# Convolution taps moved from the first two heads to later heads' maxima, and the sums across heads moved ahead of each head's filler

## The chip, the cores and the metric

The kernel runs on one core of one Trainium2 chip. The metric is device time in microseconds (us) of one execution; lower is better. The engines named below are TensorE (PE in the profile, with its weight loads as PEld), VectorE (DVE), ScalarE (ACT), GpSimd (POOL) and SyncE (SP), which issues the DMAs.

## The reference, cut to what matters

Two model blocks follow each other on 512 tokens of width 1024. The first has two layers, and each begins with a mixer that does two things to the same input and joins the results:

```python
def hybrid_mixer(x, ...):
    proj = x @ w_in + b_in
    c_q, c_kv, k_r, u = ...
    y_att = mla_group(c_q, c_kv, k_r, ...)          # 8 heads
    y_conv = conformer_conv_group(u, ...)           # 512 channels
    return concatenate([y_att, y_conv], -1) @ w_o

def mla_group(...):
    for start in range(0, S, 128):                  # causal by chunks of 64
        s = q_nope @ k_nope.T + q_rope @ k_rope.T
        p = softmax(where(mask, s * scale, -inf))
        outs.append(p @ v[:, :end])

def conformer_conv_group(u, ...):
    h = a * sigmoid(g)
    h = causal depthwise conv(h, 31 taps) + dw_b
    return silu(layer_norm(h))
```

After the mixer a layer has a cross attention over 256 memory tokens and a gated feed-forward part. The second block has a modulated mixer and a mixture of 16 experts. The change touches only the stretch of each of the two layers in which the 8 heads of `mla_group` are computed.

## The kernel before, in words

Every engine has its own instruction list, written out by hand in the order in which the engine runs it, and the lists meet through counting semaphores. An instruction that waits holds back all that stands behind it in its engine's list. Nothing reorders the work: what the code says first is done first.

In the attention stretch a head h has four query tiles t of 128 rows. Its work goes around the engines like this:

- PE, `scores(h)` (L1432): four products into four PSUM banks. From head 1 on, tile t waits until ScalarE has read the same tile of the head before.
- DVE, `maximum(n)` (L3421, L3423, L3425): a memset of the masked corner, the row maximum, and its scaled negative. After the second tile of head h, DVE does `reciprocal(h - 1)` (L3433): the reciprocals of the softmax sums of the head before.
- ACT, `exps(h)` (L2538): the exponentials with their row sums.
- PE, `turn_probs(h, tiles)` (L1443): transposes of the probabilities; ACT `turned_probs` (L2558) copies them out of PSUM.
- PE, `sums_across(pair)` (L1454): spreads the reciprocals of two heads (2 x pair and the next) over bank 4. It waits for DVE's reciprocals of both heads. ACT copies the bank to `mixT` (L2573).
- PE, `values(h)` (L1466, L1471): probabilities times values, into the same bank 4. For even h it waits for that copy.
- DVE, `pair_out(pair)` (L3438, L3441): multiplies a pair's outputs by the copied reciprocals, two heads later.

PE computes scores two heads ahead: in its loop over h the list is turn, `scores(h + 2)`, a filler, turn, turn, values. The filler is work of another part that needs a place: `modulation_rows(i)` (L1495) in heads 1 to 3 of the first layer and 1 to 4 of the second (`RING_MODS` is 4 and 5), and in head 6 `memory_product(0)` (L1197), the first of the cross attention's key and value products. The rest of them, `memory_product(1)` onward, follows the last head. `modulation_turn` (L1524) and DVE's `modulation_out` (L3447) finish a modulation chunk.

DVE has a second job, the depthwise convolution: 4 channel tiles x 31 taps = 124 instructions (L3352, and L3349 for each tile's first tap), handed out by `convolve(n)` in spare places. Before the heads 77 of them are done, the last 14 without anything between (one behind the last rotated query, then `convolve(13)`); in the heads there is one behind each maximum but the first (31), and 8 + 8 come after the last head, around the last `pair_out`. PE's `conv_sum` (L1411) needs all 124; it stands behind `memory_product(5)`.

Of the kernel before, what the change touches and what calls it, by code (L numbers as in the profile page):

```python
# [24 lines left out]
ACT = mybir.ActivationFunctionType  # L25
# [166 lines left out]
def build(nc, A, out, debug=None):  # L192
    with ExitStack() as ctx:
# [6 lines left out]
        def signal(name, per):  # L200
            return Signal(sem(name), per)
# [12 lines left out]
        ps = [banks[:, i, :] for i in range(8)]  # L214
# [27 lines left out]
        def view(lo, *shape, of=None):  # L242

            n = int(np.prod(shape))
            v = (arena if of is None else of)[:, lo:lo + n]
            if len(shape) == 2:
                return v.rearrange("p (a b) -> p a b", a=shape[0])
            if len(shape) == 3:
                return v.rearrange("p (a b c) -> p a b c", a=shape[0], b=shape[1])
            return v  # L250
# [6 lines left out]
        mixT = view(MIX, KT, S)  # L257
# [129 lines left out]
        rec_mm, rec_ev = signal("reciprocals_spread", HEADS // 2), signal("reciprocals_out", HEADS // 2)  # L387
# [361 lines left out]
        def score_tile(t):  # L749
            return ps[(0, 1, 6, 7)[t]][:, 0:(t + 1) * P]  # L750
# [116 lines left out]
        def ffn_chunk(n):  # L867

            half_no, i = (n - N_FFN) // (HALF + KT), (n - N_FFN) % (HALF + KT)
            return (half_no, half_no * HALF + i, True) if i < HALF else (half_no, i - HALF, False)  # L870
# [260 lines left out]
        def _(pe):  # L1131
# [46 lines left out]
            for l in range(DEPTH):  # L1178
# [244 lines left out]
                def scores(h):  # L1423
                    pe.wait_ge(qrot.sem, qrot.at(l, h + 1))
                    for t in range(ST):
                        n = h * ST + t
                        if n == 0:
                            pe.wait_ge(kv_ev.sem, kv_ev.at(l, 12))
                            pe.wait_ge(kcopy.sem, kcopy.at(l, 1))
                        if n >= 4:  # L1430
                            pe.wait_ge(sc_exp.sem, sc_exp.at(l, n - 3))
                        pe.matmul(score_tile(t), qh[:, h, t * P:(t + 1) * P], kh[:, h, 0:(t + 1) * P],  # L1432
                                  start=True, stop=True).then_inc(sc_mm.sem, 1)

                def turn_probs(h, tiles):
                    for kt in tiles:
                        n = h * ST + kt
                        if n >= 2:
                            pe.wait_ge(pt_ev.sem, pt_ev.at(l, n - 1))
                        if kt == 0:  # L1440
                            pe.wait_ge(sc_exp.sem, sc_exp.at(l, h * ST + ST))
                        for t in range(kt, ST):
                            mm = pe.transpose(ps[2 + n % 2][:, t * P:(t + 1) * P],  # L1443
                                              probs[:, h % 2, t, kt * P:(kt + 1) * P], ident)
                        mm.then_inc(pt_mm.sem, 1)

                def sums_across(pair):
                    pe.wait_ge(sc_rec.sem, sc_rec.at(l, 2 * pair + 2))
                    if pair:
                        pe.wait_ge(pv_ev.sem, pv_ev.at(l, pair))  # L1450
                    by_head = stat[:, 3, :].rearrange("p (h t) -> p h t", h=2)
                    for t in range(ST):
                        for i in range(2):
                            mm = pe.matmul(ps[4][i * VD:(i + 1) * VD, t * P:(t + 1) * P], by_head[:, i, t:t + 1].broadcast_to([P, VD]),  # L1454
                                           ident, start=True, stop=True)
                    mm.then_inc(rec_mm.sem, 1)
# [26 lines left out]
                def modulation_rows(i, wm=None):  # L1483
                    if wm is None:
                        arrived(C_MOD + i)
                        wm = w(C_MOD + i, 0, KT, 512)
                    if i == 0 and l == 0:
                        pe.wait_ge(cond_ok, 2)
                    if i >= 1:
                        pe.wait_ge(mod_in.sem, mod_in.at(l, i))  # L1490
                    elif l >= 1:
                        pe.wait_ge(mod_in.sem, mod_in.at(l, 0))
                    for k in range(KT):
                        for g in range(4):
                            mm = pe.matmul(mod_row(l, i)[g * MOD_COLS:(g + 1) * MOD_COLS, 0:P], cond[:, k, :],  # L1495
                                           wm[:, k, g * P:(g + 1) * P], start=(k == 0), stop=(k == KT - 1))
                        if k == 0:
                            say_spent(mm)
                    mm.then_inc(mod_rows.sem, 1)
                    if i < RING_MODS[l]:  # L1500
                        give_back(1 if i + 1 < RING_MODS[l] else 1 + MOD_CHUNKS - RING_MODS[l])
# [32 lines left out]
                for h in range(HEADS):  # L1534
                    turn_probs(h, (0, 1))
                    if h + 2 < HEADS:
                        scores(h + 2)
                    if 1 <= h < RING_MODS[l]:
                        modulation_rows(h)
                    if h == HEADS - 2:  # L1540
                        pe.wait_ge(sc_exp.sem, sc_exp.at(l, (HEADS - 1) * ST + 1))
                        memory_product(0)
                    turn_probs(h, (2,))
                    if h % 2 == 0:
                        sums_across(h // 2)
                    turn_probs(h, (3,))
                    values(h)
                    if h < RING_MODS[l]:
                        modulation_turn(h)
# [112 lines left out]
                for n in range(N_FFN, SPLIT_CHUNKS):  # L1662
                    half_no, t, hidden_tile = ffn_chunk(n)
# [706 lines left out]
        def _(act):  # L2370
            A1 = nc.scalar.activation
# [36 lines left out]
            for l in range(DEPTH):  # L2408
# [143 lines left out]
                def turned_probs(h, tiles):  # L2552
                    for kt in tiles:
                        n = h * ST + kt
                        act.wait_ge(pt_mm.sem, pt_mm.at(l, n + 1))
                        if h >= 1 and kt == 0:
                            act.wait_ge(pv_mm.sem, pv_mm.at(l, h))
                        nc.scalar.activation(probsT[:, kt, kt * P:S], ps[2 + n % 2][:, kt * P:S], ACT.Copy)\  # L2558
                            .then_inc(pt_ev.sem, 1)

                act.wait_ge(kcopy.sem, kcopy.at(l, 1))
                exps(0)
                for h in range(HEADS):
                    if h + 1 < HEADS:
                        exps(h + 1)
                    turned_probs(h, (0, 1))
                    if h < RING_MODS[l]:
                        act.wait_ge(mod_rows.sem, mod_rows.at(l, h + 1))
                        A1(gates[:, h % 2, 0:P], mod_row(l, h)[:, 0:P], ACT.Copy).then_inc(mod_row_ev.sem, 1)
                    turned_probs(h, (2,))  # L2570
                    if h % 2 == 0:
                        act.wait_ge(rec_mm.sem, rec_mm.at(l, h // 2 + 1))
                        A1(mixT[:, h // 2, :], ps[4][:, :], ACT.Copy).then_inc(rec_ev.sem, 1)  # L2573
                    turned_probs(h, (3,))
                    if h == HEADS - 2:
                        memory_copy(0)
# [145 lines left out]
                for n in range(N_FFN, SPLIT_CHUNKS):  # L2722
                    half_no, t, hidden_tile = ffn_chunk(n)
# [440 lines left out]
        def _(dve):  # L3164
# [31 lines left out]
            for l in range(DEPTH):  # L3196
# [163 lines left out]
                def convolve(n):  # L3360


                    for _ in range(n):
                        some = [t for t in range(open_tiles[0]) if taps_done[t] < TAPS]
                        others = [t for t in some if t != last_tile[0]] or some
                        t = max(others, key=lambda t: (TAPS - taps_done[t], -t))
                        tap(t)
                        last_tile[0] = t
# [37 lines left out]
                for h in range(HEADS):  # L3406
                    dve.wait_ge(up_mm.sem, up_mm.at(l, h + 1))
                    V.tensor_tensor(qh[turn, h, :], ps[h][turn, :], rope_cs[turn, :], ALU.mult).then_inc(qrot.sem, 1)
                    convolve(1)
                convolve(13)  # L3410
                def centred(t):
                    V.scalar_tensor_tensor(out=mixT[:, CT + t, :], in0=ps[5][:, :], scalar=-1.0 / CW,
                                           in1=mixT[:, CT + t, :], op0=ALU.mult, op1=ALU.add).then_inc(ccen.sem, 1)
# [36 lines left out]
                for h in range(HEADS):  # L3450
                    if h >= 4 and h % 2 == 0:
                        pair_out(h // 2 - 2)
                    for t in range(ST):
                        maximum(h * ST + t)
                        if t == 1 and h >= 1:
                            reciprocal(h - 1)
                        if h or t:
                            convolve(1)
                    if 2 <= h < RING_MODS[l] + 2:
                        modulation_out(h - 2)  # L3460
                pair_out(HEADS // 2 - 2)
# [103 lines left out]
                for n in range(N_FFN, SPLIT_CHUNKS):  # L3565
                    half_no, t, hidden_tile = ffn_chunk(n)
# [451 lines left out]
```

## Time and profile before

| what | us |
|---|---|
| median of 3 runs | 2466.85 |
| lowest, highest | 2466.54, 2467.28 |
| the profiled execution's own time | 2467.34 |
| span of the profile | 2465.5 |
| PE, DVE, ACT busy in the span | 2408.1, 1245.4, 792.9 |

The profile is one execution; its times count from the span's start. The heads of the first layer lie between about 111 and 183 us, those of the second between about 885 and 959 us. An engine's timeline shows each instruction's start and duration, its line and operation, and in brackets how long the engine had been idle before it and who ended that. The chain of waits goes back from the last instruction through whatever released each step. A busy PE is not PE at its peak, since matmuls overlap and their ends are modelled.

### The profile page before, as it was taken

The page shows a single profiled execution, that of the slowest core. Times are in us where ns is not written, and L with a number is a line of the kernel's source. Part 1 is how long each engine was busy: PE and PEld are TensorE (multiplying, and loading weights), DVE is VectorE, ACT ScalarE, POOL GpSimd, SP SyncE. Part 2 cuts the span into 40 slices and gives each one's busy share as a digit, 9 for nine tenths or more (in the row PEclk, how much of TensorE's full clock was granted, in tenths as well). Part 3 has the DMA queues.
Part 4 walks back from the last instruction along what each step waited for, and adds up shares of the span by engine and source line. Part 5 has one row for each costly group of instructions (what it writes and reads, how often), then busy time and mean ns, then how long its engine had stood idle before and what let it go on. Part 6 is the DMA issues. An engine that isn't in the chain of part 4 may idle for free.

```text
span 2465.5 us, 35670 instructions
## 1 busy us (share of the span) xinstructions
PE 2408.1 (98%) x15406; PEld 1717.3 (70%) x15406; DVE 1245.4 (51%) x1826; ACT 792.9 (32%) x1284; POOL 173.6 (7%) x117
## 2 busy tenths in 40 slices
PE   9999999999999999999999999999999999999998
PEld 6566877888887757687788888787899754444332
DVE  6983746433336896455633434687566431112222
ACT  4452434212224343353422322526332431111111
POOL 0000000000000000000000000190344010000000
PEclk9999999999999999999999999999999989999999
DMA  4342222323334233322332332311100279999998
GB/s 171 98 172 102 71 101 69 94 86 104 103 110 140 65 136 138 103 69 86 103 97 82 105 95 83 96 70 69 37 3 3 112 303 426 427 427 427 427 427 341
DMA packets 248820, 380.70 MB, mean 154 GB/s; under 512 B 21946, under 2 KB 187095, under 8 KB 224983
## 3 DMA queue, kind: packets, MB, share of 16 engines
q1 hardware_dynamic: 248316, 378.31, 41.8%
q8 instruction: 122, 2.00, 0.3%
q14 instruction: 36, 0.29, 0.0%
q10 hardware_dynamic: 346, 0.11, 0.0%
HBM read 376.28 MB, written 2.10 MB: 153 GB/s over the span
## 4 chain that ended last, share of the span: by engine, by line
PE 86%; DVE 7%; DMA 4%; ACT 2%; issue 1%; SPq 0%; DVEq 0%; ACTq 0%
PE banks L1263 40%; PE banks L2242 11%; PE banks L1197 4%; PE banks L1752 4%; PE banks L1896 4%; PE banks L1246 2%; DVE arena L3352 2%; DMA ring<-in_w_gate 2%; PE banks L2088 2%; PE banks L1617 1%; PE banks L1250 1%; PE banks L1591 1%; DMA arena<-in_w_gate 1%; PE banks L2226 1%; PE banks L2188 1%
## 5 line engine op out<-in xcount | busy, mean ns | idle before, releaser
L2612 ACT ACTIVATE w_hi<-ring 128x2048 fp32r<-128x2048 f32 (+1 forms) x100 | 174.6, 1746 | 423.9 <-PE banks L1263 423.9
L1263 PE MATMUL banks<-ffn_x_hi,w_hi 128*128 128x512 f32 x640 | 249.0, 389 | 0.0
L1263 PE MATMUL banks<-ffn_x_lo,w_hi 128*128 128x512 f32 x640 | 249.0, 389 | 0.0
L1263 PE MATMUL banks<-ffn_x_hi,w_lo 128*128 128x512 f32 x640 | 249.0, 389 | 0.0
L3211 DVE TENSOR_TENSOR w_lo<-ring,w_hi 128x2048 fp32r<-128x2048 f32 (+1 forms) x96 | 198.6, 2069 | 76.6 <-ACT w_hi L2612 75.4
L3352 DVE SCALAR_TENSOR_TENSOR arena<-arena,taps 128x512 f32<-128x512 f32 x240 | 175.0, 772 | 1.1
L3572 DVE TENSOR_TENSOR squares<-gates,banks 128x512 f32<-128x512 f32 x44 | 30.3, 688 | 275.5 <-PE banks L1263 262.3
L1263 PE MATMUL banks<-ffn_hidden_hi,w_hi 128*128 128x512 f32 x352 | 138.4, 393 | 0.0
L1263 PEld LDWEIGHTS banks<-ffn_x_lo,w_hi 128*128 128x128 f32 x640 | 120.1, 188 | 25.1
L1263 PEld LDWEIGHTS banks<-ffn_x_hi,w_lo 128*128 128x128 f32 x640 | 120.1, 188 | 24.9
L1263 PEld LDWEIGHTS banks<-ffn_x_hi,w_hi 128*128 128x128 f32 x640 | 120.1, 188 | 24.8
L1263 PE MATMUL banks<-ffn_hidden_hi,w_lo 128*128 128x512 f32 x352 | 137.1, 389 | 0.0
L1263 PE MATMUL banks<-ffn_hidden_lo,w_hi 128*128 128x512 f32 x352 | 137.0, 389 | 0.0
L3968 DVE SCALAR_TENSOR_TENSOR gates<-gates,tap_rows,banks 128x512 f32<-128x512 f32 x16 | 12.0, 747 | 231.3 <-PE banks L2242 200.0
L2242 PE MATMUL banks<-arena,zT 128*64 128x512 f32 x448 | 104.6, 604 | 2.1 <-DMA arena<-in_w_gate 1.0
L2242 PE MATMUL banks<-ring,zT 128*64 128x512 f32 x432 | 98.3, 596 | 2.0 <-DMA ring<-in_w_gate 1.6
L1197 PE MATMUL banks<-arena,ring 128*128 128x256 f32 (+1 forms) x352 | 98.0, 438 | 0.0
L1197 PEld LDWEIGHTS banks<-arena,ring 128*128 128x128 f32 x352 | 66.6, 190 | 30.6 <-issue 24.3
L1896 PE MATMUL banks<-arena 64*64 64x64 f32 x2688 | 85.8, 219 | 0.7 <-ACT arena L2883 0.7
L1896 PEld LDWEIGHTS banks<-arena 64*64 64x64 f32 x2688 | 81.9, 135 | 5.0 <-issue 1.5
L2242 PEld LDWEIGHTS banks<-arena,zT 128*64 128x64 f32 x448 | 31.0, 138 | 66.4 <-issue 59.9
L1263 PEld LDWEIGHTS banks<-ffn_hidden_lo,w_hi 128*128 128x128 f32 x352 | 66.1, 188 | 14.0 <-issue 0.5
(571 smaller groups left out, 4693.8 us busy)
## 6 DMA issues: line engine op xcount, KB each, us to landing
ring<-in_ffn_w_in SPq DMA_DIRECT2D x88, 512.0 KB, 4.7
arena<-in_w_gate SPq DMA_DIRECT2D x28, 1024.0 KB, 20.3
arena<-in_w_up SPq DMA_DIRECT2D x28, 1024.0 KB, 20.7
ring<-in_w_gate SPq DMA_DIRECT2D x27, 1024.0 KB, 21.5
ring<-in_w_up SPq DMA_DIRECT2D x27, 1024.0 KB, 20.8
ring<-in_w_down SPq DMA_DIRECT2D x24, 1024.0 KB, 16.8
arena<-in_w_down SPq DMA_DIRECT2D x24, 1024.0 KB, 19.6
ring<-in_w_mod SPq DMA_DIRECT2D x18, 1024.0 KB, 6.7
```

The costliest lines, as they stand in the source:

```text
L1197: mm = pe.matmul(bank[0:m, 0:width], weights(k), rhs(k), start=(k == 0), stop=(k == n - 1))
L1246: pe.matmul(ps[outs[o]][:, :], weights(o, wp, k), rhs[0][:, k, :], start=(k == 0 and wp == 0), stop=False)
L1250: mm = pe.matmul(ps[outs[o]][:, :], weights(o, 0, k), rhs[1][:, k, :], start=False, stop=(k == KT - 1))
L1263: mm = pe.matmul(bank[:, :], weights(wp, k), rhs(rp, k), start=(k == 0 and wp == rp), stop=(k == n - 1 and wp == 1))
L1752: mm = pe.matmul(out, wt[:, k, :], z[:, k, :], start=(k == 0 and i == 0), stop=(k == KT - 1 and i == 2))
L1896: mm = pe.matmul(units_of(bank)[rows, un, :], lhsT(un, rows), rhs(un, rows), start=True, stop=True)
L2088: mm = pe.matmul(bank, w_parts[wp], r_parts[rp], start=(k == DH and wp == rp), stop=(k == DH - 1 and wp == 1))
L2242: mm = pe.matmul(out, tokens, weights[:, n * 512:(n + 1) * 512], start=first, stop=last)
L2612: nc.scalar.activation(hi[:, 0:m], raw[n % 2][:, 0:m], ACT.Copy).then_inc(f_hi.sem, 1)
L3211: ins = V.tensor_tensor(lo[:, 0:m], raw[n % 2][:, 0:m], hi[:, 0:m].bitcast(F32), ALU.subtract)
L3352: ins = V.scalar_tensor_tensor(out=acc, in0=x, scalar=c, in1=acc, op0=ALU.mult, op1=ALU.add)
L3572: V.tensor_tensor(whole, gates[:, t % 2, :], ps[2 * (t % 4) + 1][:, :], ALU.mult)\
```

## The change

It does two things. First, taps: `convolve(13)` ahead of the heads becomes `convolve(10)`; head 0 (three taps) and head 1 (four) lose the taps between their maxima; every head from 1 on gets two taps behind its four maxima. What is left after the last head falls from 8 + 8 to 6 + 6. The number of taps, 124, stays. Second, for heads 2, 4 and 6 `sums_across` moves up in PE's list, from behind the third transposed tile to right behind `scores(h + 2)`, which is ahead of the filler; ACT's copy of it moves up ahead of the copy of the modulation row. Head 0 keeps the old order.

```diff
@@ PE, loop over the heads
                     turn_probs(h, (0, 1))
                     if h + 2 < HEADS:
                         scores(h + 2)
+                    if h % 2 == 0 and h:
+                        sums_across(h // 2)
                     if 1 <= h < RING_MODS[l]:
                         modulation_rows(h)
                     if h == HEADS - 2:
                         pe.wait_ge(sc_exp.sem, sc_exp.at(l, (HEADS - 1) * ST + 1))
                         memory_product(0)
                     turn_probs(h, (2,))
-                    if h % 2 == 0:
-                        sums_across(h // 2)
+                    if h == 0:
+                        sums_across(0)
                     turn_probs(h, (3,))
                     values(h)
@@ ACT, loop over the heads
+                def sums_copy(pair):
+                    act.wait_ge(rec_mm.sem, rec_mm.at(l, pair + 1))
+                    A1(mixT[:, pair, :], ps[4][:, :], ACT.Copy).then_inc(rec_ev.sem, 1)
...
                     turned_probs(h, (0, 1))
+                    if h % 2 == 0 and h:
+                        sums_copy(h // 2)
                     if h < RING_MODS[l]:
...
                     turned_probs(h, (2,))
-                    if h % 2 == 0:
-                        act.wait_ge(rec_mm.sem, rec_mm.at(l, h // 2 + 1))
-                        A1(mixT[:, h // 2, :], ps[4][:, :], ACT.Copy).then_inc(rec_ev.sem, 1)
+                    if h == 0:
+                        sums_copy(0)
                     turned_probs(h, (3,))
@@ DVE, ahead of the heads
                     convolve(1)
-                convolve(13)
+                convolve(10)
@@ DVE, loop over the heads
                         maximum(h * ST + t)
                         if t == 1 and h >= 1:
                             reciprocal(h - 1)
-                        if h or t:
+                        if h >= 2:
                             convolve(1)
+                    if h:
+                        convolve(2)
                     if 2 <= h < RING_MODS[l] + 2:
                         modulation_out(h - 2)
                 pair_out(HEADS // 2 - 2)
                 reciprocal(HEADS - 1)
```

On PE, at head 6 of both layers (L1443 are the transposes, L1454 the sums across heads, L1197 `memory_product(0)`, L1466 the values):

```order
 L1443 MATMUL banks<-consts,zT 128x128 [waits probsT_ev]
 L1443 MATMUL banks<-consts,zT 128x128 x2
+L1454 MATMUL banks<-consts,stat 64x128 [waits pv_ev,sums_reciprocal]
+L1454 MATMUL banks<-consts,stat 64x128 x7
 L1197 MATMUL banks<-arena,ring 128x256 [waits slot1_loaded,scores_exp]
 L1197 MATMUL banks<-arena,ring 128x256 x7
 L1443 MATMUL banks<-consts,zT 128x128 [waits probsT_ev]
 L1443 MATMUL banks<-consts,zT 128x128
-L1454 MATMUL banks<-consts,stat 64x128 [waits pv_ev,sums_reciprocal]
-L1454 MATMUL banks<-consts,stat 64x128 x7
 L1443 MATMUL banks<-consts,zT 128x128 [waits probsT_ev]
 L1466 MATMUL banks<-arena 64x128 [waits probsT_ev,reciprocals_out]
```

The wait for the reciprocals now stands ahead of the memory product instead of behind it. Head 2 of both layers and head 4 of the second have the same shift around `modulation_rows`.

On DVE, the end of head 7 before (L3421 to L3425 are a maximum, L3352 a tap, L3438 and L3441 `pair_out(2)`, L3433 the last reciprocal, on which the fourth sums across heads waits):

```order
L3421 MEMSET banks 64x64
L3423 TENSOR_REDUCE stat<-banks 128x1
L3425 TENSOR_SCALAR stat<-stat 128x1
L3352 SCALAR_TENSOR_TENSOR arena<-arena,taps 128x512
L3438 TENSOR_TENSOR arena<-arena,banks 128x384
L3441 TENSOR_TENSOR arena<-arena,banks 64x128 x2
L3433 RECIPROCAL stat<-stat 128x4
L3352 SCALAR_TENSOR_TENSOR arena<-arena,taps 128x512 x8
```

and now (all line numbers are 7 higher):

```order
L3428 MEMSET banks 64x64
L3430 TENSOR_REDUCE stat<-banks 128x1
L3432 TENSOR_SCALAR stat<-stat 128x1
L3359 SCALAR_TENSOR_TENSOR arena<-arena,taps 128x512 x3
L3445 TENSOR_TENSOR arena<-arena,banks 128x384
L3448 TENSOR_TENSOR arena<-arena,banks 64x128 x2
L3440 RECIPROCAL stat<-stat 128x4
L3359 SCALAR_TENSOR_TENSOR arena<-arena,taps 128x512 x6
```

Two more taps stand ahead of the last reciprocal in this head, as in every head from 2 on.

## Rows read from the trace of the kernel before

**Rows 1.** The page's chain that ended last, share of the span by engine.

```profile
PE 86%; DVE 7%; DMA 4%; ACT 2%; issue 1%; SPq 0%; DVEq 0%; ACTq 0%
```

**Rows 2.** Chain of waits, first layer, heads 0 to 2: start us, us, what.

```profile
111.23 9.37 DVE arena L3352 x14
...
134.10 1.12 PE banks L1454 x16
135.24 0.61 ACT arena L2573
...
149.83 1.05 PE banks L1454 x16
```

**Rows 3.** Chain of waits, first layer, head 6: start us, us, what.

```profile
172.87 3.46 PE banks L1197 x16
...
176.54 1.05 PE banks L1454 x16
...
178.26 0.32 PE banks L1466
```

**Rows 4.** Timeline of PE, first layer, heads 0 and 1: start us, us, what, idle before.

```profile
119.84 2.40 PE L1432 MATMUL banks<-arena 128*128 128x128 f32 x8 [0.73 <-issue]
...
124.05 1.57 PE L1432 MATMUL banks<-arena 128*128 128x128 f32 x6
```

**Rows 5.** Timeline of DVE, first layer, heads 2 to 7.

```profile
131.91 0.11 DVE L3421 MEMSET banks<- 64x64 f32 x1
...
138.73 0.11 DVE L3421 MEMSET banks<- 64x64 f32 x1 [0.74 <-PE banks L1432]
...
153.36 0.17 DVE L3447 TENSOR_TENSOR mod<-banks,par 128x8 f32<-128x8 f32 x1 [1.39 <-PE banks L1524]
154.39 0.11 DVE L3421 MEMSET banks<- 64x64 f32 x1 [0.86 <-PE banks L1432]
...
160.43 0.55 DVE L3438 TENSOR_TENSOR arena<-arena,banks 128x384 f32<-128x384 f32 x1
...
161.60 0.11 DVE L3421 MEMSET banks<- 64x64 f32 x1
...
168.33 0.11 DVE L3421 MEMSET banks<- 64x64 f32 x1 [0.70 <-PE banks L1432]
...
175.45 0.18 DVE L3433 RECIPROCAL stat<-stat 128x4 f32<-128x4 f32 x1
```

**Rows 6.** Timeline of DVE, second layer, heads 3 to 7.

```profile
912.85 0.11 DVE L3421 MEMSET banks<- 64x64 f32 x1 [0.73 <-PE banks L1432]
...
927.48 0.17 DVE L3447 TENSOR_TENSOR mod<-banks,par 128x8 f32<-128x8 f32 x1 [1.40 <-PE banks L1524]
928.51 0.11 DVE L3421 MEMSET banks<- 64x64 f32 x1 [0.86 <-PE banks L1432]
...
951.31 0.18 DVE L3433 RECIPROCAL stat<-stat 128x4 f32<-128x4 f32 x1
```

**Rows 7.** Chain of waits, second layer, heads 6 and 7: start us, us, what.

```profile
952.40 1.05 PE banks L1454 x16
...
954.12 0.32 PE banks L1466
```

**Rows 8.** Stretches: A:B us, length, busy (count) of PE, PEld, DVE, ACT, POOL; PEclk, DMA share, GB/s.

```profile
127.00:131.00 4.00, 2.59 (x14) 1.55 (x12) 3.82 (x12) 1.25 (x5) 0.00 (x0) 1.00 0.77 267
131.00:135.00 4.00, 2.47 (x21) 1.43 (x20) 3.79 (x14) 2.20 (x6) 0.00 (x0) 1.00 0.02 6
...
1984.00:1986.00 2.00, 0.82 (x5) 0.73 (x5) 1.93 (x5) 2.00 (x5) 1.62 (x2) 0.50 0.94 385
...
1988.00:1990.00 2.00, 2.00 (x12) 2.00 (x11) 1.93 (x3) 0.69 (x3) 1.80 (x1) 0.55 0.37 49
```

**Rows 9.** Timeline of PE in the second block, between 1980 and 1992 us.

```profile
1980.31 3.96 PE L2166 MATMUL banks<-consts,gates 2*128 2x2 f32 x16 [1.99 <-ACT gates L2974]
1985.45 6.02 PE L2172 MATMUL banks<-consts 128*128 128x128 f32 x34 [1.18 <-DVE stat L3911]
```

## Prediction, made before the changed kernel was run

> **What bounds the kernel now.** I read the chain of waits first: PE holds 86% of it and DVE 7% [rows 1]. Most of what PE holds is steady matmul work that the change leaves alone, so what counts is who holds the chain in the two attention stretches. In the first layer it runs over DVE's 14 taps from 111.23 to 120.60, over the maxima of heads 0 and 1 with a tap between each two, to PE's first sums across heads at 134.10 [rows 2]. So DVE paces PE until there. From then on PE mostly holds the chain, and DVE waits for it: the reader is to see the bracketed idle times in DVE's timeline, 0.74 + 1.39 + 0.86 + 0.70 = 3.69 us from head 3 to head 7 of the first layer [rows 5]. In the second layer the 0.73 comes once, the pair 1.40 and 0.86 twice: 5.25 us [rows 6]. These waits are all the room that DVE has in the later heads. At head 6 the reader is to see that PE does `memory_product(0)` at 172.87, for 3.46 us, and that the fourth sums start behind it at 176.54 [rows 3], 1.1 us after DVE began the last reciprocal at 175.45 [rows 5]. That product is what hides DVE's lateness there.
>
> **Prices.** A tap in a run costs 9.37 / 14 = 0.67 us [rows 2]. A head of DVE with four taps lasts from 161.60 to 168.33 less 0.70 of idle: 6.03 us. `pair_out` takes from 160.43 to 161.60: 1.17 us [rows 5]. The four maxima and a reciprocal without taps are then 6.03 - 4 x 0.67 = 3.35 us. With two more taps a head costs 7.37 us.
>
> **The early heads, a gain.** Three fewer taps in the run end it at 118.6 instead of 120.6, but PE starts the first scores only at 119.84 [rows 4], so head 0's maxima begin at about 120.2, 0.4 us earlier. Without taps they take 3.3 us, to 123.5. Head 1's scores stand behind the first modulation rows and start at 124.05 [rows 4], so DVE waits until about 124.35, is done at 127.7, adds two taps and begins head 2 at 129.05, where it began at 131.91 [rows 5]. That is 2.9 us earlier, and since head 1's reciprocal follows two maxima later, the first sums start at about 131.2, not at 134.10 [rows 2]. ACT follows each maximum at once and isn't in the way. The second layer has the same rows 774.12 us later (154.39 against 928.51 [rows 5, 6]), so I use the first layer's times for both.
>
> **The later heads, a loss on DVE.** Twelve more taps lie between 129.05 and the last reciprocal: 8.0 us. DVE walks from there in steps of 7.37, with 1.17 for each `pair_out`: head 3 at 136.4, head 4 at 144.95, end of it 152.3. Now the moved sums count. Those of head 2 need the reciprocal of head 3, which DVE gives two maxima into head 4 (two maxima, a tap and the reciprocal: 2.1 us), so at 147.05. Before, from these sums at 149.83 [rows 2] to head 5's first maximum at 154.39 [rows 5] it took 4.56 us; now the modulation rows (1.9 us) and two transposes (0.3) follow behind the sums and the wait for ACT's copy (about 0.45, from the copy at 135.24 of 0.61 us [rows 2] less one transpose) is gone: 6.3 us. Head 5 starts at 153.35 and DVE waits 1.0 us for it. Then 153.35 + 7.37 + 1.17 = 161.9 for head 6, 169.25 for head 7, and 169.25 + 7.37 + 1.17 = 177.8 for the last reciprocal, which was at 175.45. In the second layer head 4 still has a filler behind its sums, so head 7 gets its scores 6.3 us after the sums at 161.9 + 2.1 = 164.0, at 170.3: the last reciprocal is at 178.85, or 952.97 on the second layer's clock, where it was at 951.31 [rows 6].
>
> **Where the lateness lands.** The fourth sums stand ahead of `memory_product(0)` now. PE comes to them at about 173, as it came to the product at 172.87 [rows 3], and stands still until 177.9: a wait of nearly 5 us (about 4 in the second layer) with nothing to do behind it, for the product, the transposes and the values are all in the same list. After it come the sums 1.05, the product 3.46 and three transposes 0.33, and the values of head 6 start at 182.7, not at 178.26 [rows 3]: 4.4 us later. In the second layer 953.05 + 4.84 = 957.9 against 954.12 [rows 7]: 3.8 us later. So the gain of 2.9 at the start and three copy waits of 0.45 are there, and are more than paid back. What follows the heads has the same lists, and PE paces it, so the 8.2 us stay. The taps left over, 12 with one `pair_out`, take DVE 9.2 us, under the five products of 3.46 ahead of `conv_sum`: no cost there, and the copy moved on ACT costs nothing since ACT only waits in that place.
>
> **TensorE's clock.** The trace of before has no wait of PE this long. It shows one of 1.99 us at 1980.31, followed by tiny products and another of 1.18 [rows 9], and the granted clock at 0.50, the level of 1.2 GHz, when work resumed at 1985.45; it is 0.55 on the mean from 1988 to 1990 [rows 8], so it rose at about 1989.8. Some 4.35 us at half clock cost 2.2 us. On the other side, between 127 and 135 PE was busy for 5.06 of 8 us, in pieces, and the clock stayed at 1.00 [rows 8]. The new waits are longer than the first of these and lie in denser work. Bounds: 0, and 4.4 for a fall in both layers. I take one fall, 2.2, midway, since neither row is clearly nearer. The Trainium skill's page "TensorE: Matmul & The Clock Gate", in "Part 1: The HAM clock gate", has the clock drop to 1.2 GHz when the engine has been idle and come back with sustained work. By that rule both long waits would be followed by a fall; it is the third rival.
>
> **The sum.** 8.2 + 2.2 = 10.4 us on the profiled execution's 2467.34; the median of the runs is 0.49 lower, so 2466.85 + 10.4 gives 2477.2.
>
> **Rivals.** First, DVE keeps up and the change is **faster**. The place is the last reciprocal: if it came before PE reaches the fourth sums, at 172.87 less the 2.9 us gained, nothing would be paid back, and each layer would keep 2.9 + 3 x 0.45 = 4.25 us: 2458.4. It decides from a reciprocal at 170.0 on. Against it: 129.05 plus the same work as before (175.45 - 131.91 - 3.69 = 39.85) is 168.9 without one added tap, and the twelve cost 8.0. For it only that the early gain may be larger than I read. Chance 0.05.
>
> Second, about **no change**: DVE loses all its waits and more of the taps run under them. With no idle at all the last reciprocal of the first layer comes at 168.9 + 8.0 = 176.9, and head 6's values 4.94 us later, a shift of 3.6. In the second layer head 2 began at 131.91 + 774.12 = 906.03, and DVE's work up to the last reciprocal is 951.31 - 906.03 - 5.25 = 40.03 [rows 6]; so it comes at 906.03 - 2.86 + 40.03 + 8.0 = 951.2, and the shift is 2.0 [rows 7]. Without a fall of the clock 5.6 us in sum make 2472.4. With another microsecond gained in the early heads it would be within the 0.2% (4.9 us, about what a measurement of this kernel can tell from no change). Chance of ending within it 0.12.
>
> Third, **the clock falls after both long waits**, and perhaps after the 2.4 us that PE waits at the sums of head 2 as well: 8.2 + 4.4 = 12.6, to 14.8 with one more: 2479.5 to 2481.7. Their length against the 1.99 us of before speaks for it [rows 9], the dense work around them, as between 127 and 135, against [rows 8]. Chance 0.25.
>
> **Numbers.** The forecast, late reciprocals with at most one fall, has 0.58. The range runs from 2471, a little under the second rival's price, to 2482, the top of the third; outside lie the first rival and the better half of the second. Faster 0.05, same 0.12, slower 0.83.
>
> **What would show it.** In the changed profile the first sums of each layer should start 2.9 us earlier, DVE should have one wait of 1 us (two in the second layer) from head 2 to head 7 instead of four and five, the sums of heads 2, 4 and 6 should each be released by L3440, with PE idle about 2.4, 1.8 and 4 to 5 us before them, and the values of head 6 should start 4 us late. It is wrong if PE's wait at head 6 is under 2 us, or if the time after the heads doesn't keep the shift.

## The result and the profile after

| | us |
|---|---|
| before, median of 4 runs | 2466.69 (2465.77 to 2467.28) |
| after, median of 4 runs | 2482.12 (2480.98 to 2484.11) |
| ratio, 95% interval | 1.0064 (1.0046 to 1.0081) |
| profiled execution of after, its span | 2484.11, 2482.3 |

The change makes the kernel slower by 15.4 us. The direction is the one forecast. The time lies just above the range of 2471 to 2482, and the 2477.2 are 5 us short.

The busy times hardly move. PE is busy for 5.3 us more than before, and DVE's time stands where it stood:

```profile
PE 2413.4 (97%) x15406; PEld 1724.5 (69%) x15406; DVE 1245.5 (50%) x1826; ACT 792.0 (32%) x1284; POOL 173.7 (7%) x117
```

So PE does the same instructions, some of them slower, and waits longer. The view of PE's waits says on what (columns: engine, tile and line, releaser; us in total, times, longest). Of before:

```profile
PE banks L1454 <- DVE stat L3433: 1.6, 3, 0.6
```

Of after:

```profile
PE banks L1454 <- DVE stat L3440: 20.2, 8, 4.8
```

All eight sums across heads now wait for a reciprocal, for 20.2 us in all. The next view, PE's timeline of after, first layer, shows where. Its rows answer to [rows 2, 3, 4].

```profile
119.68 2.40 PE L1432 MATMUL banks<-arena 128*128 128x128 f32 x8 [0.73 <-issue]
...
131.38 1.09 PE L1454 MATMUL banks<-consts,stat 128*64 128x128 f32 x16 [1.30 <-DVE stat L3440]
...
147.33 1.80 PE L1454 MATMUL banks<-consts,stat 128*64 128x128 f32 x16 [2.47 <-DVE stat L3440]
...
165.88 1.09 PE L1454 MATMUL banks<-consts,stat 128*64 128x128 f32 x16 [1.86 <-DVE stat L3440]
...
179.72 1.97 PE L1454 MATMUL banks<-consts,stat 128*64 128x128 f32 x16 [4.77 <-DVE stat L3440]
...
191.44 0.43 PE L1466 MATMUL banks<-arena 128*64 128x128 f32 x2
```

The first sums start 11.70 us after the first scores, where it was 14.26. Then PE stands still for 2.47, 1.86 and 4.77 us ahead of the sums of heads 2, 4 and 6. Two of these four sums last nearly twice as long as the other two, 1.80 and 1.97 us against 1.09. The second layer has the same three waits (its rows answer to [rows 7]):

```profile
932.28 1.69 PE L1454 MATMUL banks<-consts,stat 128*64 128x128 f32 x16 [2.46 <-DVE stat L3440]
...
950.83 1.09 PE L1454 MATMUL banks<-consts,stat 128*64 128x128 f32 x16 [1.86 <-DVE stat L3440]
...
965.75 1.09 PE L1454 MATMUL banks<-consts,stat 128*64 128x128 f32 x16 [4.15 <-DVE stat L3440]
966.77 5.38 PE L1197 MATMUL banks<-arena,ring 128*128 128x256 f32 x16
```

Here `memory_product(0)` (L1197) takes 5.38 us. The windows of after, in the columns of [rows 8], tell why such rows are long: PEclk, the share of TensorE's full clock that was granted, is the first number behind POOL's.

```profile
145.00:147.00 2.00, 0.00 (x0) 0.00 (x0) 1.87 (x7) 0.00 (x0) 0.00 (x0) 1.00 0.00 0
147.00:149.00 2.00, 1.67 (x16) 1.40 (x16) 1.91 (x7) 0.00 (x0) 0.00 (x0) 0.64 0.00 0
149.00:151.00 2.00, 2.00 (x42) 1.80 (x44) 1.93 (x5) 0.60 (x1) 0.00 (x0) 0.51 0.03 8
151.00:153.00 2.00, 2.00 (x43) 1.56 (x36) 1.48 (x3) 0.95 (x4) 0.00 (x0) 1.00 0.00 0
...
179.00:181.00 2.00, 1.28 (x12) 1.28 (x14) 1.96 (x6) 0.00 (x0) 0.00 (x0) 0.50 0.03 8
181.00:183.00 2.00, 2.00 (x11) 1.47 (x8) 2.00 (x4) 0.60 (x1) 0.00 (x0) 0.50 0.00 0
183.00:185.00 2.00, 2.00 (x6) 1.58 (x5) 0.61 (x1) 0.00 (x0) 0.00 (x0) 0.50 0.00 0
185.00:187.00 2.00, 2.00 (x11) 1.70 (x11) 0.00 (x0) 0.00 (x0) 0.00 (x0) 0.97 0.00 0
```

Ahead of head 2's sums PE is idle and the clock still granted in full; as work resumes it falls to 0.50, which is the level of 1.2 GHz. At head 6 it is at 0.50 by the time work resumes. It is back some 4 us after the resumption at head 2 and somewhat over 5 us at head 6. I call this a fall of the clock. What it lengthens is read from the chain of waits of after:

```profile
147.33 1.80 PE banks L1454 x16
149.13 2.79 PE banks L1495 x64
...
179.72 1.97 PE banks L1454 x16
181.69 5.35 PE banks L1197 x16
...
932.28 1.69 PE banks L1454 x16
933.97 2.90 PE banks L1495 x64
...
965.75 1.09 PE banks L1454 x16
966.84 5.31 PE banks L1197 x16
```

The same pieces at full clock stand in the chain of waits of `e8_fill_head6`, an experiment below that has this order and these taps, and no fall in the heads:

```profile
147.27 1.09 PE banks L1454 x16
148.37 1.88 PE banks L1495 x64
...
178.06 1.09 PE banks L1454 x16
179.15 3.65 PE banks L1197 x16
```

Against these the four falls add 1.62, 2.58, 1.62 and 1.66 us: 7.5.

To compare kernels I use the **length of the heads**: from the start of the first scores, the first L1432 row of a layer, to the end of its last L1466 row, the values of head 7. It is 191.44 + 0.43 - 119.68 = 72.19 us in the first layer of after. Before, it ended with this row of PE's timeline, so 182.83 - 119.84 = 62.99:

```profile
182.40 0.43 PE L1466 MATMUL banks<-arena 128*64 128x128 f32 x2
```

| | first layer | second layer | both, against before |
|---|---|---|---|
| before | 63.0 | 64.7 | |
| after | 72.2 | 72.3 | +16.8 |

The spans of the two profiles differ by 2482.3 - 2465.5 = 16.8 us too, so all of it comes from the heads (the medians of the runs are 15.4 apart). In all the profiles shown here the rest of the program, whose code no kernel changes but for the taps behind the heads, was between 2333 and 2344 us long in sum (the clock falls there too, not in the same places each time: it is 0.50 from 1760 to 1762 us in after and 1.00 over the same work in before, at 1742 to 1746), so totals can differ by several us for reasons outside the heads. The lengths of the heads are free of that.

### The profile page after: what moved, and what is told of

Read it like the earlier page. It is cut to its first block, busy times and chain, and to the rows that moved or that the text cites. A ratio compares the mean times of both kernels' runs of the same rounds, so it can differ in the third digit from the quotient of the medians.

```text
span 2482.3 us, 35670 instructions
## 1 busy us (share of the span) xinstructions
PE 2413.4 (97%) x15406; PEld 1724.5 (69%) x15406; DVE 1245.5 (50%) x1826; ACT 792.0 (32%) x1284; POOL 173.7 (7%) x117
## 4 chain that ended last, share of the span: by engine, by line
PE 86%; DVE 6%; DMA 5%; ACT 2%; issue 1%; SPq 0%; DVEq 0%; ACTq 0%
PE banks L1263 40%; PE banks L2244 10%; PE banks L1197 7%; PE banks L1754 4%; PE banks L1898 4%; DMA ring<-in_w_gate 3%; PE banks L1246 2%; PE banks L2090 2%; DVE arena L3359 1%; PE banks L1619 1%; PE banks L1250 1%; PE banks L1593 1%; DMA arena<-in_w_gate 1%; DVE stat L3430 1%; PE banks L2190 1%
## 5 line engine op out<-in xcount | busy, mean ns | idle before, releaser
L2619 ACT ACTIVATE w_hi<-ring 128x2048 fp32r<-128x2048 f32 (+1 forms) x100 | 174.6, 1746 | 423.9 <-PE banks L1263 423.9
L1263 PE MATMUL banks<-ffn_hidden_hi,w_lo 128*128 128x512 f32 x352 | 137.1, 389 | 0.0
L1197 PE MATMUL banks<-arena,ring 128*128 128x256 f32 (+1 forms) x352 | 101.5, 450 | 0.0
L1197 PEld LDWEIGHTS banks<-arena,ring 128*128 128x128 f32 x352 | 69.0, 197 | 32.0 <-issue 24.8
L1263 PEld LDWEIGHTS banks<-ffn_hidden_hi,w_hi 128*128 128x128 f32 x352 | 66.1, 188 | 14.0 <-issue 0.5
```

Of the source, the lines that this page charges most:

```text
L1197: mm = pe.matmul(bank[0:m, 0:width], weights(k), rhs(k), start=(k == 0), stop=(k == n - 1))
L1263: mm = pe.matmul(bank[:, :], weights(wp, k), rhs(rp, k), start=(k == 0 and wp == rp), stop=(k == n - 1 and wp == 1))
L2619: nc.scalar.activation(hi[:, 0:m], raw[n % 2][:, 0:m], ACT.Copy).then_inc(f_hi.sem, 1)
```

## The experiments

Theory: PE's waits cost about what the forecast says, and the clock's falls behind them cost nearly as much again. Rivals: the added taps alone, or the moved sums alone, do it; or the falls only accompany the waits and cost nothing of their own. A kernel's difference is against the runs of before that shared its chip: medians of 2468.32 (22 runs) for the first four, 2467.53 (15 runs) for the next four, 2466.82 (7 runs) for the last two.

**One part alone.** First the moved sums and their copy with before's taps, `e1_order_only`, against after:

```diff
-                convolve(10)
+                convolve(13)
@@
-                        if h >= 2:
+                        if h or t:
                             convolve(1)
-                    if h:
-                        convolve(2)
```

> The sums across heads and their copies ahead of the filler in heads 2, 4 and 6, with the taps where they were before. Theory (the place of the sums in PE's list costs by itself, for at head 6 the memory product no longer covers DVE's last reciprocal): PE waits 2.8 us at head 6 in each layer and about 0.5 us at heads 2 and 4, the three copy waits of 0.45 us go, 1.8 us later per layer, 3.7 us in all without the clock; if the clock falls after the wait at head 6, another 1.9 to 2.8 us per layer, 2470 to 2476. Rival (the moved taps alone are to blame, the order saves the copy waits): 2.7 us faster than before, 2464.

Measured: 2475.15 us (5 runs), ratio 1.0035 (1.0022 to 1.0048): 6.8 us slower. PE's timeline at head 6:

```profile
176.47 1.97 PE L1454 MATMUL banks<-consts,stat 128*64 128x128 f32 x16 [2.82 <-DVE stat L3440]
178.37 4.32 PE L1197 MATMUL banks<-arena,ring 128*128 128x256 f32 x16
```

The order is enough to make a wait at head 6, 2.82 us in each layer, and a fall behind each. So the moved sums lose even with the taps where they were. How much is not settled by this run alone: the heads of its profile are 10.5 us longer than before's, but it has two more falls, among heads 0 to 2, where its lists are those of before (the last section shows one).

Then the taps alone with before's order, `e2_taps_only`, against before:

```diff
-                convolve(13)
+                convolve(10)
@@
-                        if h or t:
+                        if h >= 2:
                             convolve(1)
+                    if h:
+                        convolve(2)
```

> The changed kernel's taps with the order of the sums from before. Theory: the last reciprocal is 2 us later as in the changed kernel, but the memory product covers all but 1 us of it and the modulation rows cover the wait of head 2; the first sums still start 2.9 us earlier; no wait is over 2.2 us, so no fall of the clock: first layer 0.2 us later, second 1.8 us earlier, 2465. Rival (late taps are the cause wherever the sums stand): at least half of the 15 us stays, over 2474.

Measured: 2465.83 us (10 runs), ratio 0.9998 (0.9988 to 1.0007): no difference. PE's timeline shows the cover at work, the product ahead of the sums:

```profile
173.25 3.62 PE L1197 MATMUL banks<-arena,ring 128*128 128x256 f32 x16
...
178.19 1.09 PE L1454 MATMUL banks<-consts,stat 128*64 128x128 f32 x16 [1.10 <-DVE stat L3433]
```

The later taps make DVE late, but the product hides all but 1.10 us of it, and about that much the early heads give back: the heads of both layers are 1.0 us longer than before's. The expectation that no clock would fall did not hold. One fall is in this profile, among heads 0 to 2 of the first layer, where the longest idle time of PE ahead of it is 1.30 us:

```profile
133.00:135.00 2.00, 1.78 (x12) 1.44 (x13) 1.93 (x5) 2.00 (x9) 0.00 (x0) 0.56 0.30 28
```

Each part by itself costs 6.8 and about 0 us, and both together 15.4: the taps make DVE late, and the order turns its lateness into waits.

**The place at head 6.** `e3_head6_late` is after with the sums and their copy of head 6 in the old place:

```diff
-                    if h % 2 == 0 and h:
+                    if h in (2, 4):
                         sums_across(h // 2)
@@
-                    if h == 0:
-                        sums_across(0)
+                    if h in (0, 6):
+                        sums_across(h // 2)
```

(and the same for `sums_copy`).

> The changed kernel with the sums and the copy of head 6 alone in their old place; heads 2 and 4 keep the new order. Theory: the waits of 4.8 and 4.2 us at head 6 shrink to 1.2 and 0.4 us and the clock doesn't fall there, while the wait of 2.5 us at head 2 and its fall (1.7 us per layer) stay: 1.5 us from the waits and 3.3 us from the clock over before, 2471 to 2472. Rival (heads 2 and 4 carry the loss too, through DVE being late for everything behind): 2476 or more.

Measured: 2472.17 us (10 runs, 2467.86 to 2478.93), ratio 1.0021 (1.0009 to 1.0034). That is 3.9 us over before in place of 15.4, so some 11 us hang on the sums of head 6; the lengths of the heads agree (133.9 us in both layers of this profile, 144.5 in after's). The fall at head 2 is still there, in both layers, behind 2.46 us of idle.

**The clock by itself.** The next three kernels are after with PE kept at work through a wait: products of a constant with itself, into columns of bank 5 that nobody reads, just ahead of the sums. They are shorter than the waits, so no sum starts more than 0.1 us later for them. `e4_fill_waits` has 9 ahead of head 2's sums and 16 ahead of head 6's:

```diff
+                    if h in (2, 6):
+                        pe.wait_ge(mod_in.sem, mod_in.at(l, min(h, RING_MODS[l])))
+                    for _ in range({2: 9, 6: 16}.get(h, 0)):
+                        pe.matmul(ps[5][:, 2 * P:3 * P], ident, ident, start=True, stop=True)
                     if h % 2 == 0 and h:
                         sums_across(h // 2)
```

> The changed kernel with products of a constant by itself ahead of the moved sums, 9 at head 2 and 16 at head 6 of both layers, written to columns of bank 5 that nobody reads; they run while PE would wait for the reciprocal and end before it. Theory (half of the loss is the clock): the sums start when they did, but PE's clock stays at 1.00, the sums take 1.05 us and the memory product 3.46 us, and about 8 us of the 15 go: 2474 to 2476. Rival (the wait alone is the loss, the clock's fall lies beside it): the time stays within 1.5 us of the changed kernel's, 2481 to 2483.

Measured: 2474.43 us (6 runs, four between 2472.30 and 2474.46 and two at 2482.49 and 2482.99), ratio 1.0038 (1.0021 to 1.0054). Work that computes nothing makes the kernel 9 us faster than after: 6.1 over before in place of 15.4. The rival, by which falls cost nothing of their own, falls. The profiled execution is one of the two long ones. Its heads, 139.0 us in both layers, are still 5.5 shorter than after's. It has no fall at heads 2 and 6 but one at head 4 of the first layer and one among heads 0 to 2 of the second, and its program behind the second layer's heads took 5 us more than after's.

`e8_fill_head6` has the same with `{6: 16}`.

> The changed kernel with 16 products of a constant ahead of the sums of head 6 alone (columns of bank 5 that nobody reads). Theory: the falls at head 6 go, 2.8 and 1.9 us, those after the wait of 2.5 us at head 2 stay: 2477 to 2478. Rival (the falls have nothing to do with the wait ahead of them): 2481 to 2483.

Measured: 2473.28 us (10 runs), ratio 1.0024 (1.0015 to 1.0034): 4 us below what was expected. The expectation left head 2's falls in; this profile shows none, though PE waited there for 2.46 us in both layers. PE's timeline around head 6 (L1541 are the added products; lines from the sums on are shifted by 4):

```profile
173.11 3.74 PE L1541 MATMUL banks<-consts 128*128 128x128 f32 x32
...
178.06 1.09 PE L1454 MATMUL banks<-consts,stat 128*64 128x128 f32 x16 [1.21 <-DVE stat L3444]
```

and its windows:

```profile
174.00:178.00 4.00, 2.85 (x26) 2.66 (x24) 3.91 (x10) 1.65 (x4) 0.00 (x0) 1.00 0.44 164
178.00:182.00 4.00, 3.94 (x30) 3.44 (x31) 3.95 (x7) 0.60 (x1) 0.00 (x0) 1.00 0.00 0
```

No clock falls in these heads, so their lengths, 68.0 and 69.1 us, tell what the waits alone cost, less what the early heads gain: 137.1 - 127.7 = 9.4 us. After has 16.8; the other 7.4 are the falls, as the rows above added up to 7.5. The median of the runs is only 5.7 us over before's, and the rest of the program is 4.2 us shorter in this profile than in before's (2333.5 against 2337.8), with some 10 us at 0.50 there against 17; so the medians don't price the falls, and the lengths of the heads do.

`e9_fill_head2` has `{2: 9}` alone.

> The changed kernel with 9 products of a constant ahead of the sums of head 2 alone, none at head 6. Theory (a wait of over 4 us is always followed by a fall of the clock, one of 2.5 us only in some executions): both falls at head 6 stay, 2.8 and 1.9 us, the waits stay as they are, and the time is 1 to 4 us under the changed kernel's on the same chip, well above the kernel with head 6 filled: 2478 to 2481. Rival (head 2's falls cost as much as head 6's): it comes down by half of what filling both did, to 2477 or less.

Measured: 2479.38 us (4 runs), ratio 1.0046 (1.0029 to 1.0063), 12.6 us over before. Both falls behind head 6's waits are there, both of head 2's are gone, and 2.8 of the 15.4 us with them. (One fall among heads 0 to 2 of the second layer is in this profile too.)

**The same kernel once more.** `e10_after_again` is after, unchanged, on another occasion.

> The changed kernel as it is, on the chip of the run that fills head 2, for a comparison on one chip and for a second look at where the clock falls. Theory: 2480 to 2483, both waits of head 6 followed by a fall again, those of head 2 perhaps. Rival (the falls of the first profile were chance at head 6 too): a wait of 4 us or more with the clock at 1.00 behind it.

Measured: 2482.17 us (4 runs), ratio 1.0058 (1.0043 to 1.0073). PE's timeline at head 2:

```profile
147.28 1.09 PE L1454 MATMUL banks<-consts,stat 128*64 128x128 f32 x16 [2.46 <-DVE stat L3440]
```

and at head 6:

```profile
179.05 1.42 PE L1454 MATMUL banks<-consts,stat 128*64 128x128 f32 x16 [4.15 <-DVE stat L3440]
180.40 5.03 PE L1197 MATMUL banks<-arena,ring 128*128 128x256 f32 x16
```

Both falls behind head 6 come again. Behind head 2's 2.46 us there is one in the second layer and none in the first, where it was in the profile above; a fourth is at head 4 of the first layer.

**The lateness removed.** If DVE's taps are what makes PE wait, fewer of them in the heads must make both orders fast, since the rest fits behind the heads. `e5_fewer_taps` has `e3_head6_late`'s order, no tap in heads 0 and 1, three a head in heads 2 to 5 and two in the last two:

```diff
-                        if h >= 2:
+                        if h >= 2 and t >= (1 if h < 6 else 2):
                             convolve(1)
-                    if h:
-                        convolve(2)
```

> The changed kernel with fewer taps in the heads: none in heads 0 and 1, three per head in heads 2 to 5, two in heads 6 and 7, the rest (34) behind the last head; the sums of heads 2 and 4 in the new place, those of head 6 in the old. Theory (the early gain is real and is paid back only by the taps that stand ahead of the reciprocals): DVE is ahead of PE from head 3 on, every sum finds its reciprocal there, the 2.9 us of the early heads, 0.9 us of the first sums and the copy waits of heads 2 and 4 are kept: 5.8 to 6 us per layer, 2455 to 2456; no fall of the clock. Rival (taps pushed behind the last head hold up the convolution's sum or the split of the mixed halves): the gain is lost there, 2463 to 2468.

Measured: 2455.59 us (5 runs), ratio 0.9949 (0.9936 to 0.9961): 11.9 us faster than before. DVE's timeline has the last reciprocal at 168.69, where PE now waits for nothing, and the 34 taps behind it in two runs:

```profile
168.69 0.18 DVE L3440 RECIPROCAL stat<-stat 128x4 f32<-128x4 f32 x1
168.78 11.32 DVE L3359 SCALAR_TENSOR_TENSOR arena<-arena,taps 128x512 f32<-128x512 f32 x17
...
181.20 11.35 DVE L3359 SCALAR_TENSOR_TENSOR arena<-arena,taps 128x512 f32<-128x512 f32 x17
...
198.67 1.89 DVE L3419 SCALAR_TENSOR_TENSOR arena<-banks,arena 128x512 f32<-128x512 f32 x3 [2.37 <-PE banks L1411]
```

Even so, DVE is ahead of `conv_sum` and waits 2.37 us for PE there.

`e6_fewer_taps_old_order` has these taps in before's order.

> The kernel before with the same fewer taps (ten ahead, none in heads 0 and 1, three per head in 2 to 5, two in 6 and 7, the rest behind the last head) and all sums in the old place. Theory: the early gain alone, 4.3 us per layer, 2458, and PE waits 0.44 us for the copy in each pair as before; the difference to the same taps with the moved sums, 2.5 to 3 us, is what the new place is worth when DVE is early. Rival (the new place is a loss by itself): this one is the faster of the two.

Measured: 2457.62 us (5 runs), ratio 0.9960 (0.9946 to 0.9974). With DVE early, the lengths of the heads put the new order of heads 2 and 4 ahead by 2.2 us (117.3 against 119.4); the two kernels' times, 2.0 us apart, overlap.

`e7_no_late_taps` is after with every sum in its new place, head 6's too, and three taps a head in heads 2 to 5 alone (`if 2 <= h < 6 and t >= 1`).

> The changed kernel with all its moved sums (head 6 too), no taps in heads 0, 1, 6 and 7, three per head in heads 2 to 5, the rest behind the last head. Theory: without taps in heads 6 and 7 the last reciprocal comes within half a microsecond of PE's arrival even ahead of the memory product, so the place of the sums that cost 4 to 5 us in the changed kernel costs nothing, 6 us per layer, 2454 to 2456. Rival (at head 6 the place is bad whatever DVE does, since pair_out stands ahead of the reciprocal): PE still waits over 1.5 us there and it is 3 us or more slower than with the sums of head 6 in the old place.

Measured: 2455.74 us (4 runs), ratio 0.9950 (0.9936 to 0.9964). PE's timeline at head 6:

```profile
168.20 1.09 PE L1454 MATMUL banks<-consts,stat 128*64 128x128 f32 x16 [0.56 <-DVE stat L3440]
```

So the place that cost some 11 us in after costs nothing to be measured when the reciprocal is there in time. All three kernels with fewer taps beat both before and after.

## Why the prediction was wrong in its time and right in its direction

- **The early heads.** A gain of 2.9 us was forecast; the first sums come 2.56 earlier. Head 1's first score tile and the way to its maximum took a little longer than the 0.30 that was taken. The chain of waits of after, head 1:

```profile
123.97 0.43 PE banks L1432 x2
124.40 0.07 issue
124.47 0.12 DVE banks L3428
```

- **The later heads.** PE's waits came out as the last part of the forecast has them: about 2.4, 1.8 and 4 to 5 us, each released by L3440, and measured 2.47, 1.86 and 4.77 (second layer 2.46, 1.86, 4.15). DVE's timeline of after, first layer, answers to [rows 5]:

```profile
154.14 0.17 DVE L3454 TENSOR_TENSOR mod<-banks,par 128x8 f32<-128x8 f32 x1 [1.66 <-PE banks L1524]
...
155.17 0.11 DVE L3428 MEMSET banks<- 64x64 f32 x1 [0.87 <-PE banks L1432]
...
179.49 0.18 DVE L3440 RECIPROCAL stat<-stat 128x4 f32<-128x4 f32 x1
```

  Four waits have become one place with two, 1.66 + 0.87 = 2.53 us where 1.0 was forecast, and the last reciprocal is 1.7 later than the 177.8 worked out. The fall at head 2, which the walk left out, stretches PE's sums and modulation rows by 1.62 us, and what DVE waits for comes behind them. Where no clock fell, `e8_fill_head6`, the sums of head 6 start at 178.06, against 177.9 forecast.
- **Where the lateness lands.** Right: in the idle time ahead of head 6's sums, with nothing behind it to do. `e2_taps_only` shows the cover that was there and `e3_head6_late` what its loss costs. The waits' term was 8.2 us; `e8_fill_head6` gives 9.4. The sums came back to the end in full: what follows the heads keeps the shift.
- **TensorE's clock: this is the step that failed.** The forecast took "one fall, 2.2, midway", with bounds of 0 and 4.4 "for a fall in both layers". There were four, one behind each wait at heads 2 and 6 of both layers. The price of one was nearly right: 7.5 / 4 = 1.9 us. With the waits' 9.4 they give the 16.8 of the profiles within 0.1, where the forecast had 8.2 + 2.2 = 10.4: 1.2 of what it lacked are the waits, 5.3 the clock. The number was wrong twice. The text had a reason for none and for one in each layer, and none for a single one; it was an average. And the upper bound counted one wait a layer, though the same text had a wait of 2.4 us at head 2, longer than the 1.99 us of its own nearest row [rows 9]. (That row was also read loosely: in before's windows the clock is 1.00 from 1980 to 1982 and 0.74 on the mean from 1982 to 1984, so it fell some 2.7 us after that wait had ended, while PE did the tiny products.) The third rival named both; it allowed three falls, 2481.7, and came nearest.
- What [rows 8] were taken to say, that dense work around an idle stretch keeps the clock up, doesn't hold for waits of 2.46 us and more, of which thirteen of sixteen were followed by a fall; the rows show pauses of about a microsecond each, and the last section shows that even those are no safe ground. By the rule of the Trainium skill's "TensorE: Matmul & The Clock Gate", in "Part 1: The HAM clock gate", both long waits, those at head 6, would be followed by a fall; the traces agree, with a fall at all six waits of over 4 us.

Left open: why the same wait of 2.46 us is followed by a fall in one execution and not in another. The rows ahead of it show no difference, and no run here settles it.

## What to carry to other kernels

Before a wait is moved ahead of filler work, find out whether its releaser is there by then: if it is late, the filler was what hid it, and the whole of the lateness becomes idle time. Price such idle time of TensorE twice, once for the wait and once for the falls of the clock that can follow, counting every wait and not one a layer: here a fall cost 1.6 to 2.6 us and came behind all eight waits of 2.8 us and more in the heads, and behind five of the eight of 2.46. The better cure was to take work away from the releasing engine and put it where that engine waits anyway: with fewer taps ahead of the reciprocals the kernel is 10 to 12 us faster, in either place of the sums.

## What was not expected of the hardware

A wait of 2.46 us was followed by a fall in five of the eight places where it stands (after both layers, `e3_head6_late` both, `e10_after_again` one of two, `e8_fill_head6` none). Waits of 2.82 us were in two of two (`e1_order_only`), those of 4.1 to 4.8 us in six of six. Of the twelve waits of 1.86 or 1.87 us two were, at head 4 of the first layer in `e4_fill_waits` and in `e10_after_again`, whose windows show it:

```profile
167.00:169.00 2.00, 2.00 (x11) 1.13 (x8) 1.97 (x5) 1.43 (x6) 0.00 (x0) 0.50 1.05 410
```

The same place in after, with 1.86 us of idle, has the clock at 1.00. Nor is a wait of that length needed. The windows of `e1_order_only`, over a stretch of [rows 8]:

```profile
131.00:135.00 4.00, 3.12 (x9) 1.36 (x10) 3.78 (x14) 2.11 (x6) 0.00 (x0) 0.60 0.00 0
```

PE has the same scores and the same pauses there as before, up to 1.03 us each, and the clock is 0.60 in place of 1.00. The second layer of this profile has the same, and `e2_taps_only`, `e4_fill_waits` and `e9_fill_head2` have one such fall each among heads 0 to 2, with no idle time of PE over 1.30 us ahead of it in the heads. So whether a pause of 1 to 2.5 us costs a fall differs between executions; it is one likely reason, which no run tried, why the runs of `e3_head6_late` lie between 2467.86 and 2478.93 us. It is not the only one: the longest of them is the profiled one, and outside the heads it is 5.4 us longer than before.
